# The first loads put in the order of use, and sum steps split around weight tiles, in a two-block transformer kernel

## The reference

```
c_act = silu(c)
for layer in range(2):
    mod = (c_act @ ada_w[layer] + ada_b[layer])      # 1024 -> 6 x 1024
    sh1, sc1, g1, sh2, sc2, g2 = split(mod, 6)
    h = rms_norm(x, norm1_g[layer]) * (1 + sc1) + sh1
    mix = even_mixer(h, even_w_in, ...) if layer == 0 else odd_mixer(h, odd_w_in, ...)
    x = x + g1 * mix
    h = rms_norm(x, norm2_g[layer]) * (1 + sc2) + sh2
    x = x + g2 * grouped_moe(h, router, 16 experts)
# second stack, each layer: a mixer, then attention over a memory, then a gated feed-forward
    mem_n = rms_norm(mem, mem_norm_g[layer])
    k, v = mem_n @ ca_wk[layer], mem_n @ ca_wv[layer]
```

## Time and profile before

| | us |
|---|---|
| median of three runs | 1930.87 |
| the runs | 1930.87, 1922.32, 1932.16 |
| the profiled execution | 1924.69 |
| its span, first to last instruction | 1922.9 |
| TensorE busy | 1781.6 |
| VectorE busy | 1264.2 |
| ScalarE busy | 1072.3 |

### The profile page before, as it was taken

How to read it: one execution, slowest core, us unless ns; L and a number is a source line. 1 busy time by engine, 2 the same in 40 slices (tenths; PEclk the granted TensorE clock), 3 DMA queues, 4 the chain that set the end, 5 groups by cost and what they waited for, 6 DMA issues and landing times.

```text
span 1922.9 us, 26992 instructions
## 1 busy us (share of the span) xinstructions
PE 1781.6 (93%) x9505; PEld 1474.0 (77%) x9505; DVE 1264.2 (66%) x2000; ACT 1072.3 (56%) x1649; POOL 13.8 (1%) x29
## 2 busy tenths in 40 slices
PE   5897799999999999999999999888999998889998
PEld 4785478888886866888888688566999876669997
DVE  5686658889885756589888653755545555655454
ACT  2443247888873454578878553555444454564443
POOL 1000000000000000000000000000000000000000
PEclk9998799999999999899999999798999998999999
DMA  9876738899993935399999744122566562215652
GB/s 350 294 248 215 240 105 319 319 359 355 323 355 130 330 119 188 119 354 351 325 360 344 248 147 132 45 88 66 180 192 193 171 197 66 88 44 180 192 180 83
DMA packets 217284, 413.07 MB, mean 215 GB/s; under 512 B 13120, under 2 KB 69488, under 8 KB 216800
## 3 DMA queue, kind: packets, MB, share of 16 engines
q1 hardware_dynamic: 214176, 400.74, 60.7%
q0 software_dynamic: 1904, 8.26, 1.3%
q10 hardware_dynamic: 1120, 2.97, 0.4%
HBM read 410.87 MB, written 1.05 MB: 214 GB/s over the span
## 4 chain that ended last, share of the span: by engine, by line
PE 79%; DVE 11%; ACT 5%; issue 3%; DMA 2%; DVEq 0%; ACTq 0%; SPq 0%
PE banks L722 21%; PE banks L724 21%; PE banks L723 20%; DVE weights_low L2068 2%; PE banks L984 2%; PE banks L1126 2%; DMA weight_ring<-in_ada_w 1%; PE banks L1069 1%; DVE row_gains L2339 1%; PE banks L739 1%; PE banks L752 1%; ACT scratch L1668 1%; PE banks L779 1%; ACT weights_high L1517 1%; DVE x_state L2194 1%
## 5 line engine op out<-in xcount | busy, mean ns | idle before, releaser
L2068 DVE TENSOR_TENSOR weights_low<-weight_ring,weights_high 128x1024 fp32r<-128x1024 f32 (+1 forms) x656 | 772.1, 1218 | 186.7 <-ACT weights_high L1517 107.3
L722 PE MATMUL banks<-weights_high,features_parts 128*128 128x512 f32 (+1 forms) x1488 | 592.5, 398 | 22.2 <-DVE features_parts L2501 8.2
L723 PE MATMUL banks<-weights_low,features_parts 128*128 128x512 f32 (+1 forms) x1488 | 581.9, 391 | 0.0
L724 PE MATMUL banks<-weights_high,features_parts 128*128 128x512 f32 (+1 forms) x1488 | 581.8, 391 | 0.0
L1797 ACT ACTIVATE weights_high<-weight_ring 128x1024 fp32r<-128x1024 f32 x384 | 392.2, 1056 | 103.7 <-PE banks L724 69.3
L722 PEld LDWEIGHTS banks<-weights_high,features_parts 128*128 128x128 f32 x1488 | 282.0, 190 | 87.9 <-issue 15.7
L724 PEld LDWEIGHTS banks<-weights_high,features_parts 128*128 128x128 f32 x1488 | 281.6, 189 | 59.8
L723 PEld LDWEIGHTS banks<-weights_low,features_parts 128*128 128x128 f32 x1488 | 282.0, 189 | 55.7 <-issue 1.0
L1517 ACT ACTIVATE weights_high<-weight_ring 128x1024 fp32r<-128x1024 f32 (+1 forms) x176 | 176.1, 1043 | 139.5 <-PE banks L724 88.9
L722 PE MATMUL banks<-features_parts,weights_high 128*128 128x256 f32 x736 | 210.5, 286 | 1.7 <-DVE features_parts L2163 1.5
L723 PE MATMUL banks<-features_parts,weights_high 128*128 128x256 f32 x736 | 208.5, 283 | 0.0
(11 more groups left out here) (371 smaller groups left out, 1620.7 us busy)
## 6 DMA issues: line engine op xcount, KB each, us to landing
weight_ring<-in_exp_w_gate SPq DMA_DIRECT2D x128, 512.0 KB, 5.2
weight_ring<-in_exp_w_up SPq DMA_DIRECT2D x128, 512.0 KB, 5.1
weight_ring<-in_exp_w_down SPq DMA_DIRECT2D x128, 512.0 KB, 5.3
weight_ring<-in_ada_w SPq DMA_DIRECT2D x96, 512.0 KB, 5.2
weight_ring<-in_ffn_wg SPq DMA_DIRECT2D x44, 512.0 KB, 4.3
weight_ring<-in_ffn_wu SPq DMA_DIRECT2D x44, 512.0 KB, 4.6
weight_ring<-in_ffn_wd SPq DMA_DIRECT2D x44, 512.0 KB, 4.2
weight_ring<-in_even_w_in SPq DMA_DIRECT2D x28, 512.0 KB, 5.7
```

Of the source, the lines that this page charges most:

```text
L722: eng.matmul(dst, lh, rh, start=first, stop=False, **kw)
L723: eng.matmul(dst, lh, rl, start=False, stop=False, **kw)
L724: mm = eng.matmul(dst, ll, rh, start=False, stop=last, **kw)
L2068: V(half_of(low(s), i, size), half_of(slot(n), i, size), half_of(high(s), i, size).bitcast(F32), ALU.subtract)\
```

## The change

- SP waits for the memory's landing after the first modulation tile, then loads the first memory weight, the second tile, the second memory weight, x (from ScalarE's queue), and goes on with the other sums and memory weights.
- POOL waits for the memory's landing before its small loads. The gate biases leave these and go, with the three large late loads, behind the first high half of the first `even_in` tile. `ada_take` of sum 4 waits for them.
- Both memory transposes come first on TensorE, then keys, modulation, values, modulation for each layer. VectorE does four steps, normalises and takes both transposes, then four steps, x, and the other sums.
- Before the features of x only the first tile is split; the second tile's split comes on ScalarE after the feature take 3, on VectorE after take 5 (`midway`).
- In `project` the eight steps become four, the low halves of one tile, four, the low halves of the next. This holds for `even_in` and `odd_in`.

```diff
+            first = st["ada"][0]
+            load(first[0], cols(a["ada_w"][0], 0, 512, 0, 4), 4)
+            eng.wait_ge(mem_loaded, 16)
+            mem_weights(0, 0)
+            load(first[1], cols(a["ada_w"][0], 0, 512, 4, 4), 4)
+            loaded_chunks[0] += 1
+            mem_weights(0, 1)
+            eng.dma_start(X[:, :, :], a["x"].rearrange("b (t p) d -> p (b t) d", p=128)).then_inc(x_loaded, 16)
+            ada()
+            mem_weights(1, 0)
+            ada()
+            mem_weights(1, 1)
+            ada()
...
             turn_normed("mem0")
-            turns_taken("mem0")
-            mem_keys(0)
             turn("mem1", lambda i, tb: NB[:, tb, i * 128:(i + 1) * 128])
             turns_taken("mem1")
-            modulation((2, 3))
-            mem_values(0)
-            modulation((2, 3))
-            mem_keys(1)
-            modulation((2, 3))
-            mem_values(1)
-            modulation((2, 3))
+            for l in range(2):
+                mem_keys(l)
+                modulation((2, 3))
+                mem_values(l)
+                modulation((2, 3))
...
-            splits(tiles[st["even_in"][0][0][0]]["split"] + 2)
+            s0 = tiles[st["even_in"][0][0][0]]["split"]
+            splits(s0 + 1)
             eng.wait_ge(scales_ready, 1)
-            take_turned("a0h1", feature, lambda i: (SCL[:, 0, i:i + 1], MOD[:, 0, i:i + 1]), True)
+            take_turned("a0h1", feature, lambda i: (SCL[:, 0, i:i + 1], MOD[:, 0, i:i + 1]), True, lambda: splits(s0 + 2))
...
+                    if midway is not None and i == 5:
+                        midway()
...
                     if j in before:
-                        ada_steps(KD)
+                        ada_steps(4)
+                        splits(min(end, tiles[ts[1]]["split"] + 2))
+                        ada_steps(4)
                     splits(min(end, tiles[ts[1]]["split"] + 3))
                     between(j)
...
             eng.wait_ge(c_ready, 1)
-            ada_steps(KD)
+            ada_steps(4)
             normalise(lambda tb: PR[:, tb * D:(tb + 1) * D])
...
             take_turned("mem0", feature, lambda i: (GM[:, 10, i:i + 1], None))
-            ada_steps(KD)
             take_turned("mem1", lambda i: MEM_HT[1][:, i, :], lambda i: (GM[:, 11, i:i + 1], None))
-            ada_steps(KD)
-            ada_take(0, (2, 3))
+            ada_steps(4)
             eng.wait_ge(turned, turns["mem1"][0] + KD)
             eng.wait_ge(x_loaded, 16)
             norm_x()
             ada_steps(KD)
-            for j in (1, 2, 3):
+            for j in range(4):
                 ada_take(j, (2, 3))
-            splits(tiles[st["even_in"][0][0][0]]["split"] + 2)
+                if j < 2:
+                    ada_steps(KD)
...
+            eng.wait_ge(mem_loaded, 16)
...
-            eng.wait_ge(copied["act"], chunks[st["kv1"][1][-1]]["done"])
+            eng.wait_ge(high_ready, 2 * tiles[st["even_in"][0][0][0]]["split"] + 1)
+            eng.dma_start(GB[:, 0:2, :], a["gate_bias"][0:2].partition_broadcast(128)).then_inc(gates_loaded, 16)
             for dst, src in ((bias, a["rel_bias"]), (EARLY, a["early"]), (SCR[:, 0:RET_HEADS, :], a["decay"])):
                 eng.dma_start(dst, src).then_inc(late_loaded, 16)
```

More of the change, by code:

```diff
@@ L537, in diff_turned_at @@
             return SCRF[:, 1536 + 384 * (t % 2):1920 + 384 * (t % 2)]
-        CONSTS, MORE, LATE = 16 * 3, 16 * 8, 16 * 3
+        CONSTS, MORE, LATE = 16 * 3, 16 * 7, 16 * 3
         block = ctx.enter_context(nc.Block())
@@ L649, in cross, with mem_weights @@
                 load(st[f"cao{l}"][0], cols(a["ca_wo_2"][l], 0, D, 0, 2), 2)
[L651 to L654, removed]
+            def mem_weights(l, i):
+                w = ("ca_wk_2", "ca_wv_2")[i]
+                eng.dma_start(MEM_WEIGHTS[2 * l + i], cols(a[w][l], 0, 256)).then_inc(kv_loaded[2 * l + i], 16)
+            first = st["ada"][0]
[11 more added lines that the diff above has]
+            ada()
             for j in range(7):
@@ L1503, in _ @@
                 eng.dma_start(dst, src).then_inc(consts_loaded, 16)
-            eng.dma_start(X[:, :, :], a["x"].rearrange("b (t p) d -> p (b t) d", p=128)).then_inc(x_loaded, 16)
             at_split, parts = [0], [0]
@@ L1525, in high_features, with take_turned @@
                 eng.activation(HH[:, k:k + count, :], HT[:, k:k + count, :], ACT.Copy).then_inc(features_high, 1)
-            def take_turned(name, dst, affine=None, split=False):
+            def take_turned(name, dst, affine=None, split=False, midway=None):
                 first, items = turns[name]
@@ L1544, in take_turned @@
                         high_features(i - 1, 2, (x + 1) // 2)
+                    if midway is not None and i == 3:
+                        midway()
             features = [0]
@@ L1820, in _ @@
             take_turned("mem0", feature, lambda i: (GM[:, 10, i:i + 1], None))
-            take_chunks(st["kv0"][0], lambda c: MK[:, 0, c, :])
             take_turned("mem1", lambda i: MEM_HT[1][:, i, :], lambda i: (GM[:, 11, i:i + 1], None))
@@ L1827, in _ @@
             take_root(SS, TB, D)
-            take_chunks(st["kv0"][1], lambda c: MV[:, 0, c, :])
-            take_chunks(st["kv1"][0], lambda c: MK[:, 1, c, :])
-            take_chunks(st["kv1"][1], lambda c: MV[:, 1, c, :])
-            splits(tiles[st["even_in"][0][0][0]]["split"] + 2)
+            for l in range(2):
+                take_chunks(st[f"kv{l}"][0], lambda c: MK[:, l, c, :])
+                take_chunks(st[f"kv{l}"][1], lambda c: MV[:, l, c, :])
+            s0 = tiles[st["even_in"][0][0][0]]["split"]
+            splits(s0 + 1)
             eng.wait_ge(scales_ready, 1)
-            take_turned("a0h1", feature, lambda i: (SCL[:, 0, i:i + 1], MOD[:, 0, i:i + 1]), True)
+            take_turned("a0h1", feature, lambda i: (SCL[:, 0, i:i + 1], MOD[:, 0, i:i + 1]), True, lambda: splits(s0 + 2))
             P0 = pview(EVEN_IN)
@@ L2347, in ada_take @@
                 l, i = j // 12, j % 12
-                if j == 16:
-                    eng.wait_ge(gates_loaded, 16)
+                if j in (4, 16):
+                    eng.wait_ge(gates_loaded, 16 * (1 + j // 12))
                 if j in ADA_ON_PE:
@@ L2977, in _ @@
         def _(eng):
-            for dst, src in ((AG[:, :], a["qk_gains"]), (GB[:, 0:2, :], a["gate_bias"][0:2].partition_broadcast(128)),
-                             (RW[:, :, :], cols(a["router_w"], 0, 16)), (RB[:, :], a["router_b"].partition_broadcast(128)),
+            eng.wait_ge(mem_loaded, 16)
+            for dst, src in ((AG[:, :], a["qk_gains"]), (RW[:, :, :], cols(a["router_w"], 0, 16)), (RB[:, :], a["router_b"].partition_broadcast(128)),
                              (POS[:, :, :], a["cmp_pos"]), (W2[:, :], a["cmp_w2"]), (PI[:, :], a["positions_fm"]),
```

## The result

The changed kernel takes 1940.1 us (median of 9 runs, 1931.8 to 1951.8) where the kernel before takes 1930.3 beside it. The ratio of the timed executions, which is not the quotient of the two medians (those lie 9.8 us apart), is 1.0063, 95% interval 1.0044 to 1.0083: some 12 us slower. I had forecast 1931, so no change that can be told, with 0.74 on that and 0.13 on slower. The steps were the right ones. Four of their sizes were too small, all in the same direction.

The account below looks back on a forecast made before the run. TensorE, busy 93% of the span, was taken as the bound, its dense stages untouched. Terms -9.1 + 3.7 + 1.0 + 8.0 = +3.6 us gave 1928.3 against the profiled execution; with the timed runs, 1931 was predicted, range 1919 to 1942.

Parts of the forecast that it names:

- Part 1: Front: memory lands sooner and transposes start at 12.3 instead of 22.18; -9.1 us, bounds -11.5 to -5.
- T: Moment when VectorE takes the fourth modulation sum: 62.44 us before the change, forecast 53.3.
- I cost the later x, the moved issues on SP and the POOL wait at nothing: Front: a margin of 7 us before the fourth product asks was to absorb these delays; size 0.
- Part 3: Large late loads at the first split delay group 1's tile to T+21.2, TensorE pauses 2.4 us.
- part 2: First products: one tile split before the features, second midway; -2.3 us, TensorE starts at T+5.7, lost again by group 1.
- Part 4, the front's groups: Halved sums around a split: group 2 usable T+36.5 against T+32.8, +3.7 us; groups 4 to 6 add +1.0.
- Part 4, the odd projection: Halved sums lengthen rounds to 15.6 us; group 4 slips 2.5, group 5 6.1, slow clock +1.9; +8.0 in all.
- A' to B, p' to the next p: Ring with halved sums: next sum tile B waits for sum tile A', the next weight tile for weight tile p'.
- B lands at 3.8 and 6.4: Ring round: halves of the next sum tile land these us after the first half of A' is used; round 15.6.
- R2: Slower rival: the 15.6 us round binds from the first odd group; 17.5 instead of 8.0, +13, 1941; chance 0.11.
- R1: Faster rival: the ring covers the new order and group 1 keeps its 2.3 us; -11, 1917; chance 0.13.
- R3: Front rival: constants still end at about 16.3, so T falls by 5 only; +7.7, 1935; chance 0.12.

Follow-up runs that it names:

- the experiment on x: Changed kernel with the load of x issued one place earlier, ahead of the second memory weight: 1936.7 us, 1.0046 of the kernel before.
- matched halves: Halved sums, ring loaded in the order of use: on the kernel before (its front kept) 1927.7 us, 1.000; on the changed kernel 1920.9 us, 0.9956.
- whole sums: Changed kernel with the eight steps of a modulation sum in one piece again, in both projections: 1921.7 us, 0.996 of the kernel before.
- x first: Changed kernel with ring loads in the order of use and x loaded ahead of the second memory weight: 1914.4 us, 0.9927 of the kernel before.
- the halves alone: Kernel before with only the halved sums added, in both projections, front untouched: 1944.7 us, 1.008 of the kernel before.
- matched ring: Changed kernel, halved sums kept, ring tiles handed out and loaded in the order of use: 1920.9 us, 0.9956 of the kernel before.
- whole sums, interleaved ring: Changed kernel with sums in one piece but ring loads alternating columns and group: 1929.3 us, 1.0008 of the kernel before.

## Why the prediction was wrong, step by step

The sum was +3.6 us for a measured 12. Taken by places in the profiled pair (+16.6 behind the odd projection), the terms that missed are these:

- **Part 1, T at 53.3: measured 57.13.** The start of the transposes was right (12.81 for 12.3), and so was the landing of the memory. The step that failed is "I cost the later x, the moved issues on SP and the POOL wait at nothing". I had reckoned a margin of 7 us from the total of bytes by about 43 us. The bytes were not late; one tile was. x landed at 26.65, 15.7 us after its issue, and of the loads issued just ahead of it the second memory weight took 14.0 and a half modulation tile 11.6, so the norm and the first sum came 3 us after TensorE wanted them. The bill was 2.99 of waiting, 0.84 on the row sums (1.79 for 0.95), and 2.61 on the next keys (9.76 for 7.15): 6.4 us. That moving x alone removes it, the experiment on x shows. How large it is, is partly luck: in the five traces with this front TensorE waited 0.6 to 4.2 us there, and the fourth sum was taken at 52.0 to 57.1. A budget of bytes says when the last load is through, not when a given one is.
- **The clock behind the transposes.** I had read the earlier trace rows as showing that transposes leave the clock low. The Trainium skill ("TensorE: Matmul & The Clock Gate", Part 4: PE-mode transpose) says that transposes do not count as busy for it. The traces contradict both. In the changed kernel 32 transposes back to back take 5.74 us (5.33 to 6.52 in the others with its front), where twice the 3.65 of the earlier trace rows would be 7.3: the faster pace begins within them, with nothing but transposes before it. Behind them and 0.62 us of idle time the keys run at the high level (2.4 GHz) throughout, 7.14 us. And behind 16 transposes on the front of before they can do so too, as the matched halves there show:

```profile
22.38 3.65 PE L770 MATMUL banks<-constants,normed 128*128 128x128 f32 x16 [22.38 <-DVE normed L2138]
26.65 7.14 PE L1144 MATMUL banks<-qk_features,aux 128*128 128x256 f32 x32 [0.62 <-ACT qk_features L1557]
```

The granted clock of the windows does not help here. It reads 1.00 under the slow keys of before as well, so the pace is what tells. I had put T at 51.5 if transposes counted; with x early it is 51.3 to 52.3 in four traces. The 8.97 of one execution was chance, and a row that fits a rule need not be a test of it.
- **Part 3, group 1 at T+21.2: measured T+20.9.** The size was right and the reason only half. In the changed kernel ScalarE did wait 5.9 us for the ring tile behind the late loads. With whole sums ScalarE waits as long (5.9 us), but VectorE works through from its sum to both splits without a gap, and group 1 stands at T+20.8 all the same: there VectorE is the bound, and the late loads cost nothing. With matched halves group 1 starts at T+19.1, or T+18.8 with x first, with the same late loads: the 2.3 us of part 2 are not lost there. Part 2 itself came as forecast, T+5.7 (62.83).
- **Part 4, the front's groups: +3.7 and +1.0.** Measured -5.8 at group 1 to 0.0 at group 2, which is +5.8, and then +5.0 up to 600 instead of +1.0. Not all of the +5.0 need be the halves': whole sums drift by +1.3 over the same stretch, and two kernels with the same code there differ by some 4. Of the latter VectorE's waits over 96 to 166 show the same pattern again (6.2 us for high halves, 2.5 for columns). I had counted group 2's wait with care and treated the last even groups by a glance, though they have the same round.
- **Part 4, the odd projection: +8.0, measured +11.6.** The mechanism was as written: A' to B, p' to the next p, pauses ahead of the last groups, at a constant slip per round. Counted as I had counted it, from the first odd groups on, it is +13.2 (from +3.4 to +16.6; 13.6 with the halves alone): at the entry of the projection the profiled pair had drifted by 1.6 the other way. The size missed at "B lands at 3.8 and 6.4": the first half landed 3.7 us after issue, the second 5.8 after its own, 7.4 into the round, with three more halves issued right behind it within 1.5 us. The round is 16.8 us, not 15.6. And TensorE had less ahead of it than I took: group 3 slipped 1.1 instead of nothing, groups 4 and 5 5.2 each, the last one 1.6 more. R2, the rival that let the round bind early, had 17.5 for this term; the truth lies between them.

The rival on the faster side, R1, was right that the ring could cover the new order, but only with its loads in that order. As the kernel stood it was false. R3 did not come about: the constants landed by 10.9.

How I weighed it was wrong as well: the open costs (x, SP's moved issues, the last even groups) had all been set at or near nothing, and each could only go up. A forecast made of such terms should have leaned to slower, and the range (1919 to 1942) was wide enough only by 2 us.

## What to carry to other kernels

When a piece of work that reads a ring of buffers is cut and interleaved with another, the loads have to be cut and interleaved in the same way. A ring filled in one order and emptied in another loses its depth: here 15 to 17 us of 1930, and nothing once the loads were reordered. When loads are reordered in a saturated front, ask of each tile when it lands and who asks for it, x as well as the weights; and a wait of TensorE can cost its own length and as much again in the clock behind it (2.1 to 4.2 us of waiting cost 2.6 to 3.5 more here, and 0.6 to 0.9 us cost nothing more). One profiled execution is one draw of the clock and of the landings, so a row that is to carry a rule is worth comparing with the same row of another execution.

## What the runs showed of the hardware

- A TensorE that waited 2.99 us ran its next 32 products in 9.76 us instead of 7.15, with the granted clock at 0.83 and 0.75 over the 16 us around them. After waits of 2.10 and 4.18 us the same products took 10.10 and 8.83. After waits of 0.59 us (matched ring) and 0.94 us (whole sums, interleaved ring) they took 7.15.
- TensorE's pace rose while it ran nothing but transposes: 32 of them back to back took 5.33 to 6.52 us, where 16 at the start of TensorE's work took 3.65, and the 32 keys behind them took 7.14 or 7.15 us in all ten traces with the new front. Behind 16 transposes the keys took 8.97, 9.25 and 7.14 us in three traces.
- A load of x (1 MB) in the saturated front landed 13.5 to 16.7 us after its issue in five traces with the same code ahead of it.
- A 512 KB half issued 1.6 us behind another took 5.1 us to land in the kernel before, with the next one issued 1.6 us behind it. In the changed kernel such halves took 5.8 to 6.5 us with the next one 0.4 us behind. So a later issue seems to slow an earlier one on the same queue; no run changed this alone.
